# Triangular inverses of two delta rules: 64x64 blocks on two tiles of the array, or 32x32 blocks on four tiles joined at the end

## The reference, cut to what matters

```python
a = jnp.where(strict, jnp.einsum('bhnld,bhnsd->bhnls', kb, k) * lmask, 0.0)
t = lax.linalg.triangular_solve(a + eye, jnp.broadcast_to(eye, a.shape),
                                left_side=True, lower=True, unit_diagonal=True)
u = jnp.einsum('bhnls,bhnse->bhnle', t, v * beta[..., None])
wk = jnp.einsum('bhnls,bhnsd->bhnld', t, kb * jnp.exp(gc)[..., None])
```

## Time and profile before

| | |
|---|---|
| time, median of 3 runs | 4557.46 us (4542.09 to 4565.45) |
| the profiled execution | 4550.43 us, its span 4549.1 us |
| busy in the span | PE 4046.0 us (89%), PEld 3288.3 (72%), DVE 2075.1 (46%), ACT 1251.5 (28%), POOL 454.3 (10%) |
| mean granted TensorE clock | 0.929 of 2.4 GHz |
| instructions in the span | 75,162 |
| first delta rule with the neighbourhood attention | 668 to 1062 us of the span |
| second delta rule with the fox attention | 2802 to 3312 us |

### The profile page before, as it was taken

One profiled execution on the slowest core, in us unless ns is written; L12 is line 12 of the kernel. 1 busy time (PEld: TensorE's weight loads), 2 busy tenths in 40 slices (PEclk: granted clock), 3 DMA queues, 4 the chain that ended last, 5 costly groups with the idle time before them and its releaser, 6 DMA issues. The chain is left out here.

```text
span 4549.1 us, 75162 instructions
## 1 busy us (share of the span) xinstructions
PE 4046.0 (89%) x33230; PEld 3288.3 (72%) x33230; DVE 2075.1 (46%) x3302; ACT 1251.5 (28%) x1786; POOL 454.3 (10%) x442
## 2 busy tenths in 40 slices
PE   6999849995898899999899996878868989999979
PEld 5788727774676688888588785666656768888867
DVE  4633426554333444445513214655633365655662
ACT  4222244332222221121411214334221232222231
POOL 0001102231201000000200002232201200000010
PEclk9999869997899899999899998998967989999989
DMA  5211120113112111111122323011003211111101
GB/s 180 87 43 62 45 74 6 30 30 139 40 37 93 38 55 47 47 47 55 65 95 89 116 88 90 26 52 44 7 33 137 97 41 52 47 47 47 56 31 63
DMA packets 213687, 281.94 MB, mean 62 GB/s; under 512 B 15580, under 2 KB 170972, under 8 KB 213236
## 3 DMA queue, kind: packets, MB, share of 16 engines
q1 hardware_dynamic: 176048, 185.58, 13.0%
q10 hardware_dynamic: 37316, 91.56, 5.3%
HBM read 217.11 MB, written 60.00 MB: 61 GB/s over the span
## 5 line engine op out<-in xcount | busy, mean ns | idle before, releaser
L425 PE MATMUL ps<-sb_a_h,sb_whi 128*128 128x512 f32 (+1 forms) x3008 | 1206.1, 401 | 128.5 <-DVE sb_a_h L516 66.2
L426 PE MATMUL ps<-sb_a_h,sb_wlo 128*128 128x512 f32 (+1 forms) x3008 | 1192.3, 396 | 0.0
L427 PE MATMUL ps<-sb_a_h,sb_whi 128*128 128x512 f32 (+1 forms) x3008 | 1191.7, 396 | 0.0
L425 PEld LDWEIGHTS ps<-sb_a_h,sb_whi 128*128 128x128 f32 (+1 forms) x3008 | 575.4, 191 | 289.5 <-issue 91.4
L427 PEld LDWEIGHTS ps<-sb_a_h,sb_whi 128*128 128x128 f32 (+1 forms) x3008 | 576.7, 192 | 123.7
L426 PEld LDWEIGHTS ps<-sb_a_h,sb_wlo 128*128 128x128 f32 (+1 forms) x3008 | 578.1, 192 | 118.6 <-issue 1.0
L387 DVE TENSOR_TENSOR sb_wlo<-sb_wraw,sb_whi 128x2048 fp32r<-128x2048 f32 (+3 forms) x146 | 315.8, 2163 | 428.7 <-ACT sb_whi L379 405.0
L1850 DVE TENSOR_TENSOR sb_x<-sb_x,ps 128x512 f32<-128x512 f32 x480 | 314.4, 684 | 299.3 <-PE ps L427 299.1
L379 ACT ACTIVATE sb_whi<-sb_wraw 128x2048 fp32r<-128x2048 f32 (+3 forms) x146 | 260.4, 1784 | 678.1 <-PE ps L427 509.1
L425 PE MATMUL ps<-sb_a_g,sb_whi 128*128 128x512 f32 x896 | 349.7, 390 | 9.6 <-DVE sb_x L1850 9.6
L426 PE MATMUL ps<-sb_a_g,sb_wlo 128*128 128x512 f32 x896 | 348.6, 389 | 0.0
(11 more groups left out here) (467 smaller groups left out, 4980.5 us busy)
## 6 DMA issues: line engine op xcount, KB each, us to landing
sb_wraw<-w_in SPq DMA_DIRECT2D x33, 1024.0 KB, 5.4
sb_wraw<-w_ff SPq DMA_DIRECT2D x32, 1024.0 KB, 5.2
sb_wraw<-w_up SPq DMA_DIRECT2D x22, 1024.0 KB, 5.1
sb_wraw<-w_down SPq DMA_DIRECT2D x11, 1024.0 KB, 4.9
sb_wraw<-w_xkv SPq DMA_DIRECT2D x8, 1024.0 KB, 5.7
sb_wraw<-w_out SPq DMA_DIRECT2D x8, 1024.0 KB, 5.1
sb_a_f<-y ACTq DMA_DIRECT2D x16, 512.0 KB, 5.3
gates<-sb_a_f ACTq DMA_DIRECT2D x32, 256.0 KB, 2.0
```

The source lines that it names most:

```text
L425: e.matmul(o, wh[:, k, c], xh[:, sl], start=(k == 0), stop=False)
L426: e.matmul(o, wl[:, k, c], xh[:, sl], start=False, stop=False)
L427: m = e.matmul(o, wh[:, k, c], xl[:, sl], start=False, stop=(k == t.nk - 1))
```

## The change

Both delta rules invert only 32x32 diagonal blocks by levels 2, 4, 8 and 16, and join them to 64x64 at the end.

- A step works on 4 blocks of 32 a head (2 chunks x 2), block r on the array's tile of rows and columns 32r to 32r+31. Operands lie in a compact form of 32 columns a head (`small`), M and the final result in the old one of 64 (`wide`). Xt and Xa are the two halves of one tile XX.
- The start: 24 products turn the small blocks around and 24 more copy them, into one bank; VectorE adds the identity to both halves at once. GpSimd's step is gone.
- Each level: 24 products for Y, VectorE's mask over half as many columns, 48 products for both updates into one bank, one subtraction by VectorE.
- The join: 12 products on two off-diagonal tiles (`gd_y` 4), two negations by VectorE over 32 partitions each, then a group that assembles the 64x64 result in PSUM: 24 products with the identity, 12 with zeros, 12 for the off-diagonal block. VectorE copies it out.
- The number of steps of each generator stays 15 (TensorE's), and `gd_u`, `gd_w` and the scan are as before. In the second delta rule the numbers are 32 for 24, 64 for 48 and 16 for 12.

```diff
-LEVELS = [2, 4, 8, 16, 32]
+LEVELS = [2, 4, 8, 16]
...
+            def parts():
+                return [(r, h) for h in range(6) for r in range(4)]
+
+            def small(ap, r, h):
+                return ap[32 * r:32 * r + 32, 32 * h:32 * h + 32]
+
+            def wide(ap, r, h, s):
+                return ap[32 * r:32 * r + 32, 64 * h + 32 * s:64 * h + 32 * s + 32]
...
-                for c, h in blocks():
-                    m = e.matmul(block(ps, c, h), block(Xt, c, h), C("eye", 64 * c, 64 * c + 64), start=True, stop=True)
+                for r, h in parts():
+                    e.matmul(small(ps, r, h), wide(Xf, r, h, r % 2), eye32(r), start=True, stop=True)
+                    m = e.matmul(small(ps[:, 192:384], r, h), eye32(r), wide(Xf, r, h, r % 2), start=True, stop=True)
...
-                for lv in range(5):
-                    e.wait_ge(*bk.emptied(("gd_xa", n, lv - 1) if lv else ("gd_t", n)))
-                    pe_blocks(e, ("gd_y", n, lv), ONE_BANK, M, Xt)
+                for lv in range(4):
+                    e.wait_ge(*bk.emptied(("gd_x", n, lv - 1) if lv else ("gd_t", n)))
+                    ps = bk.take(("gd_y", n, lv), ONE_BANK)
+                    e.wait_ge(*bk.room(("gd_y", n, lv)))
+                    for r, h in parts():
+                        m = e.matmul(small(ps, r, h), wide(M, r, h, r % 2), small(Xt, r, h), start=True, stop=True)
...
-                    pe_blocks(e, ("gd_xt", n, lv), ONE_BANK, Xa, Ym)
-                    if lv < 4:
-                        pe_blocks(e, ("gd_xa", n, lv), ONE_BANK, Ym, Xa)
...
+                    for r, h in parts():
+                        e.matmul(small(ps, r, h), small(Xa, r, h), small(Ym, r, h), start=True, stop=True)
+                        m = e.matmul(small(ps[:, 192:384], r, h), small(Ym, r, h), small(Xa, r, h), start=True, stop=True)
...
+                for h in range(6):
+                    for c in range(2):
+                        m = e.matmul(small(ps, 2 * c + 1 - k, h), wide(M, 2 * c + k, h, 1 - k), small(Xt, 2 * c + k, h),
+                                     start=True, stop=True)
...
+                for r, h in parts():
+                    e.matmul(wide(ps, r, h, r % 2), eye32(r), small(Xt, r, h), start=True, stop=True)
+                    if r % 2 == k:
+                        m = e.matmul(wide(ps, r, h, 1 - k), eye32(r), wide(C(zero), r, 0, 1 - k), start=True, stop=True)
+                e.wait_ge(*bk.emptied(("gd_y", n, 4)))
+                for h in range(6):
+                    for c in range(2):
+                        o = 2 * c + 1 - k
+                        m = e.matmul(wide(ps, o, h, k), small(Xa, o, h), small(Ym, o, h), start=True, stop=True)
...
-                    e.tensor_tensor(Xt, Xt, bk["gd_xt", n, lv][:, 0:384], ALU.subtract).then_inc(*bk.empty(("gd_xt", n, lv)))
-                    if lv < 4:
-                        e.tensor_tensor(Xa, Xa, bk["gd_xa", n, lv][:, 0:384], ALU.subtract).then_inc(*bk.empty(("gd_xa", n, lv)))
-                    yield
+                    e.wait_ge(*bk.filled(("gd_x", n, lv)))
+                    e.tensor_tensor(XX, XX, bk["gd_x", n, lv][:, 0:384], ALU.subtract).then_inc(*bk.empty(("gd_x", n, lv)))
+                    yield
+                e.wait_ge(*bk.filled(("gd_y", n, 4)))
+                for c in range(2):
+                    o = slice(64 * c + 32 * d, 64 * c + 32 * d + 32)
+                    e.tensor_scalar(Ym[o, 0:192], bk["gd_y", n, 4][o, 0:192], -1.0, None,
+                                    ALU.mult).then_inc(*(bk.empty(("gd_y", n, 4)) if c else vo.up()))
+                yield
+                e.wait_ge(*bk.filled(("gd_x", n, 4)))
+                e.tensor_copy(Xf, bk["gd_x", n, 4][:, 0:384]).then_inc(*bk.empty(("gd_x", n, 4)))
...
-                e.wait_ge(*gd_x0[d].at(s))
-                e.tensor_tensor(v6(R(Xas[d], 384)), m6("eye"), v6(R(Xts[d], 384)), ALU.add).then_inc(*gd_xa0[d].up())
```

More of the change, by code:

```diff
@@ L1652, in ac_prep @@
                 if n >= 2:
[L1653 removed]
+                    e.wait_ge(*bk.emptied(("gd_x", n - 2, 4)))
                 if s >= 2:
@@ L1836, in program @@
         un_squared, un_root, un_done = sig("unit_squared"), sig("unit_root"), sig("unit_done")
-        gd_x0, gd_xa0, gd_mask, gd_dec = ([sig(f"gd_{n}{d}") for d in range(2)] for n in ("x0_", "xa0_", "mask", "decay"))
+        gd_x0, gd_mask, gd_dec = ([sig(f"gd_{n}{d}") for d in range(2)] for n in ("x0_", "mask", "decay"))
         gd_kbv, gd_faded, gd_sub, gd_twice = sig("gd_keys_values"), sig("gd_faded"), sig("gd_u_less"), sig("gd_second_pass")
@@ L2883, in pe_in @@
                 e.wait_ge(*bk.room(("rw_t", i)))
-                for c, h in blocks():
-                    m = e.matmul(block(ps, c, h), block(R(XT, 512), c, h), C("eye", 64 * c, 64 * c + 64), start=True, stop=True)
+                for r, h in parts():
+                    e.matmul(small(ps, r, h), wide(R(XF, 512), r, h, r % 2), eye32(r), start=True, stop=True)
+                    m = e.matmul(small(ps[:, 256:512], r, h), eye32(r), wide(R(XF, 512), r, h, r % 2), start=True, stop=True)
                 m.then_inc(*bk.fill(("rw_t", i)))
@@ L2898, in pe_in @@
                     yield
-                for lv in range(5):
-                    e.wait_ge(*bk.emptied(("rw_xa", i, lv - 1) if lv else ("rw_t", i)))
-                    pe_blocks(e, ("rw_y", i, lv), R(M, 512), R(XT, 512))
+                for lv in range(4):
+                    e.wait_ge(*bk.emptied(("rw_x", i, lv - 1) if lv else ("rw_t", i)))
+                    ps = bk.take(("rw_y", i, lv), ONE_BANK)
+                    e.wait_ge(*bk.room(("rw_y", i, lv)))
+                    for r, h in parts():
+                        m = e.matmul(small(ps, r, h), wide(R(M, 512), r, h, r % 2), small(XT, r, h), start=True, stop=True)
+                    m.then_inc(*bk.fill(("rw_y", i, lv)))
@@ new lines, in pe_in @@
+                    m.then_inc(*bk.fill(("rw_x", i, lv)))
+                    yield
+                e.wait_ge(*bk.emptied(("rw_x", i, 3)))
+                ps = bk.take(("rw_y", i, 4), ONE_BANK)
+                e.wait_ge(*bk.room(("rw_y", i, 4)))
+                for h in range(8):
+                    for c in range(2):
+                        m = e.matmul(small(ps, 2 * c, h), wide(R(M, 512), 2 * c + 1, h, 0), small(XT, 2 * c + 1, h), start=True, stop=True)
+                m.then_inc(*bk.fill(("rw_y", i, 4)))
@@ new lines, in pe_in @@
+                yield
+                ps = bk.take(("rw_x", i, 4), ONE_BANK)
+                e.wait_ge(*bk.room(("rw_x", i, 4)))
+                for r, h in parts():
+                    e.matmul(wide(ps, r, h, r % 2), eye32(r), small(XT, r, h), start=True, stop=True)
+                    if r % 2:
+                        e.matmul(wide(ps, r, h, 0), eye32(r), wide(C("U64"), r, 0, 0), start=True, stop=True)
+                e.wait_ge(*bk.emptied(("rw_y", i, 4)))
+                for h in range(8):
+                    for r in (0, 2):
+                        m = e.matmul(wide(ps, r, h, 1), small(XA, r, h), small(R(Y, 256), r, h), start=True, stop=True)
```

112 lines of the change are left out of this document (77 added, 35 removed).

## The result

The changed kernel takes 4692.66 us (median of 4 runs, 4683.01 to 4700.3) against 4554.18 for the kernel before: a ratio of 1.0303, 95% interval 1.0267 to 1.0339, so 138 us slower. Forecast were 4660 us and 4590 to 4750.

A forecast was written before the change was run, and what follows sets the result against it. The prediction took the fetching of TensorE's instructions to bound the changed first rule: +104 us there, +10 for load bursts, -10 in the second rule, together +104 on the profiled 4550.4 us; forecast median 4660 us, range 4590 to 4750.

The forecast's parts named there:

- the supply of instructions: First rule: instruction blocks fetched one at a time, 3.6 to 4.1 us each; 135 packets at 3.7 us, +104 us; chance 0.77.
- the price of the tiles: TensorE's groups in both rules: a pair on a 32x32 tile takes 32 ns, plus 0.15 us per change of shape.
- The line through 64, 128 and 512 columns: TensorE pair periods of 58, 110 and 430 ns, read as 0.83 ns a column and some 5 ns.
- The bursts: First rule, two bursts of input loads: a new fetch stall comes in full at each, +5 us each, +10.
- the second rule: Second delta rule: not capped on average, but local stalls and a low clock return most of the gain: -10 us.
- the array's 27 us: Second rule: TensorE's own work falls 33 us in the stage, counted as -27 because it is busy 82%.
- The rival that the clock falls too: TensorE granted 1.2 GHz for long in the first rule: another 200 us at worst, some 4760 to 4860; chance 0.07.
- 24.6 us a unit, set by TensorE: First rule before the change: 394 us for 16 units, with TensorE busy for 361 us as the bound.
- the first rival: Both rules: the supply keeps up, so TensorE's nets count, -43 - 27 = -70 us, 4487 us; chance 0.11.
- Issue in the hundreds of us: Sign of being right: TensorE's idle time for issue in the hundreds of us, in stops that end behind packets.

The follow-up runs named there:

- the first split: Kernel before, each product of the first rule's inverse groups and start's turn made as two over half the stationary columns: 4656.26 us, ratio 1.0236.
- The finer wait: Kernel before, both rules: TensorE begins the next Y once VectorE has subtracted into Xt, not also into Xa: 4527.33 us, ratio 0.9952.
- the crossed layout in both rules: Kernel before, 64x64 blocks, Xa and Y on the other chunk's partitions, so both updates run at once on four tiles: 4557.36 us, ratio 1.0014.
- The crossed layout in the first rule alone: Kernel before, first rule's updates at once on four tiles, VectorE crossing the start instead of a second bank: 4554.39 us, ratio 1.0004.

## Why the prediction was right, and where it was off

**Right: the supply of instructions bounds the changed stage.** Divided by packets, the first stage gives 5.02 us before (82, not bound by it), 4.12 with 109 packets, and 4.02, 3.99, 3.97, 4.00 and 3.99 with 123, 130, 136, 136 (the first rule alone) and 140, with tiles of three shapes, work inside and outside the delta rule, and clocks from 0.80 to 0.97. The Trainium skill ("Runtime: NRT & Kernel Launch", Instruction fetch mechanics) calls the fetch of such blocks hidden; by that rule the first split would have cost at most its changes of tile shape, which its expectation put at some 20 us, and it cost 107 us.

**Right: the price of the tiles, in part by luck.** Of the unit's parts, 48 pairs of L1618 start 0.55 us before the next group, 12 on a tile; less 0.15 for the change of shape that is 33 ns a pair, 32 were taken. (The 23 such groups at a granted clock of 1.00 all take 0.55 us, twelve at 1.2 GHz take 0.79 in the median.) The reason given, that a pair's period follows the moving columns alone, was wrong: the run with 32 moving columns on 64x64 tiles took 58 ns. The line through 64, 128 and 512 columns gave the right number for a tile that is smaller in rows and stationary columns too; which side counts was not tried.

**Off: the length of the first stage.** The sum had 135 packets at 3.7 us and +10 us for the bursts, +114 us; measured were +128 us (+129 in the run with this rule alone). The turn itself was right: 122 of 135 intervals have a mean of 3.74 us. The bursts were right too: the three long intervals that start at 840, 1013 and 1021 us, among the input loads, take 8 us more than three of 3.74. What the sum left out are the other ten long intervals, 13 us more than ten of 3.74. In six of them TensorE does not stand still once, so it was its own work that took the time there: the stage was costed as if it were capped in every packet. That the stage over its packets comes to 3.97 us is the sum of these parts, not the time of one turn.

**Off: the second rule.** I took -10 between -27 and +15; the run alone gave +14. "On the average it is not capped" held: 102 packets in 546.6 us are 5.4 us each, and TensorE's waits for issue are 23 us. The step that failed is the next one, that local stalls and a lower clock give back most of the array's 27 us: they gave back all of it, and 14 us more. How much of it was stalls and how much the clock of 0.83 stays open. The two errors are 15 and 24 us; 33 us of them show in the whole, 4693 against 4660.

**The rival that the clock falls too** is half right: it fell to 0.82 where 0.99 was, in the first stage. There it cost nothing that these runs show, since the first split, at a clock of 0.95, takes the same time for a packet; the price of 200 us was that of a TensorE that does not wait for instructions. For the second stage this is not shown.

**A premise that the runs put in doubt.** "24.6 us a unit, set by TensorE" was read from TensorE's 361 of 394 us. The finer wait took 10 us off the stage with the busy time unchanged (369.0), and the crossed layout in both rules took 42 us off the busy time and 12 off the stage: level by level, TensorE and VectorE also wait for each other's answers. The crossed layout in the first rule alone gave nothing for 36 us, but with 34 us more work for VectorE. So the first rival, an unbound supply with -43 us from TensorE's own time, might not have come about in that size either; this was not tried by itself, as no kernel of this scheme has few enough instructions. "Issue in the hundreds of us" was too high as well: 95 us in the first stage by the engine's idle time, 120 in the whole kernel.

## What to carry to other kernels

Count TensorE's instructions in each stage before cutting products into smaller ones, and divide the stage by its packets in the instruction queue: at 4.0 us a packet, as in five kernels here, the engine is fed no faster, and fewer instructions help (one product over all heads instead of one for each gave back some 60 us). A stage at 4.1 is capped in part; look at the intervals themselves. A busy share of 90% is not yet a bound: in a chain of short steps between two engines, see which single answer each step waits for, and wait for that one alone. In the whole kernel's time that was worth more here than four tiles at once, though in the first stage the two gave much the same, 10 and 12 us. A tile's price should be measured at its own shape, rows, columns and moving columns, before it is put into a sum. And a gain in the whole time should be looked for in the stage that was changed: here stages that were left alone moved by up to 11 us from kernel to kernel.

## What the hardware showed that was not expected

- TensorE's instructions come in packets of 16 KB, some 255 recorded instructions each. In the changed kernel's first stage 122 of 135 intervals are between 3.3 and 4.4 us, 3.74 in the mean; none in any run is under 3.2. TensorE stops at the same place of each packet (steps of 254, 255 and 507 recorded instructions), for 1.2 to 1.5 us in the four stops shown, even inside a group of products that waits for nothing.
- On a 64x64 tile a pair with 32 moving columns takes as long as one with 64 (58 ns); on 32x32 tiles it takes 33 ns.
- A VectorE instruction with two operands in SBUF took 0.55 us for 384 elements a row with GpSimd idle and 1.07 us with GpSimd at work beside it; those that read PSUM took 0.55 in either case.
- The clock granted was 0.80 to 0.82 in first stages full of 32x32 products (TensorE busy for 77%), and 0.95 to 0.97 with 64x32 tiles at nearly the same time for a packet (busy for 80 and 75%). The granted levels are 1.2 and 2.4 GHz; why the one stage spends more of its time at the lower was not looked into.
